# Sequence transform of a three-block model over folded rows, with its table resident, the convolution's norm moved one stage up, and context taps moved to GpSimd

## The chip, the cores and the metric

The kernel runs on one core of one Trainium2 chip. The metric is the device time of one execution in microseconds. Engines are named as in the profile: PE is TensorE, PEld its weight loads, DVE is VectorE, ACT is ScalarE, POOL is GpSimd, SP is SyncE.

## What is computed

The model has three blocks over 1024 tokens of width 1024 (a first block with two mixers and a feed-forward, then an "even" and an "odd" block), with 256 context tokens beside them in the last two. The change touches the even block's mixer alone:

```python
a_val, a_glu, a_gate, b_val, b_gate = split(h @ w_in, [512] * 5)
u = a_val * sigmoid(a_glu)
u = silu(layernorm(dwconv(u, a_conv_w) + a_conv_b, a_ln_g, a_ln_b))   # 31 taps along the tokens
y_a = (u @ a_pw_w + a_pw_b) * silu(a_gate)
y_b = fourier_mix(b_val, b_fw) * silu(b_gate)
return concat([y_a, y_b]) @ w_out

def fourier_mix(v, fw):            # v: (tokens, 4 groups, 128)
    f = fftn(v, axes=(tokens, group width), norm='ortho').real
    return einsum('blgd,gde->blge', f, fw)
```

The same runs for the 1024 tokens (`U`, `VB`) and the 256 context tokens (`UC`, `VBC`). Channels lie on the partitions, tokens along the free axis, so 512 channels are 4 tiles j.

## The kernel before

The program is a row of stages. An engine enters a stage when ACT, PE and DVE have left the one before (`gate`); POOL and SP run ahead of the gate as their own semaphores let them. Two stages matter here.

**Stage `ein`** is the projection h @ w_in: 20 units of 128 output columns. A unit's weights go as RAW through a split into a high part WH and a low part WL; the unit's matmuls (L306 for the 1024 tokens, L313 for the context) wait for WL. From unit 4 on ACT makes WH (L2266), behind its eviction of unit i-2, and POOL makes WL by one subtraction (L2278) in `ein_pool`, in the order of the units. WH and WL have two buffers each, so WL(i) can be made while unit i-1 runs, and no earlier than unit i-2 is done. Units 0 to 7 are glu and value of the four channel tiles; after unit 2j+1 DVE writes U[j] and UC[j] (L2248, L2249), then frees the unit's PSUM. Units 8 to 11 are b_val (`VB`), 12 to 15 b_gate, 16 to 19 a_gate, all evicted by ACT.

Beside this DVE runs the convolution, `conv(dve, a, b)`: for each of 4 x 31 taps q one multiply-add over 1024 tokens into ACC and one over 256 into ACCC (L2230; the first tap of a tile is L2227, the copy back L2235). It does 12 taps after each of the first three pairs of units and the other 88 after the fourth; each tap waits for the one before it.

At the end of `ein`, `val_pe` forms PQ (the 128-point transform times fw, L2367) and multiplies VB and VBC by it: 8 tiles of 128 of the 1024 tokens and 2 of context, 4 groups each, 256 columns (L2377). ACT evicts each tile in two copies (L2391) to VP_, VQ_ (the cosine and the sine side) or VPC, VQC.

**Stage `ef`**: the transform along the tokens. `DFT` lists ("a", t) for groups 0 and 1 and ("b", t) for groups 2 and 3, 8 token tiles each, then two context tiles "c". An "a" or "b" tile is 2 groups x 2 sides of a 512-column f32 matmul (L2436; each f32 matmul is two records in the trace), 64 in all. Even tokens go to one PSUM bank, odd ones to another; outputs k and k + 512 are their sum and difference, made by DVE in `group(g)`. The cosine and sine rows come from a 1024 x 1024 table in 128-row pieces over four buffers (`TAB`), each piece loaded twice, once for "a" and once for "b". In the same stage DVE, ACT and PE do the layer norm of the convolution: sums over the 4 channel tiles (L2529, `ones_sum` L1602), centring (L2534), squares by ACT (L2493), sums of these (L2541, L1602), square root (L2496), reciprocal (L2545), scaling (L2549), silu (L2501). `group(g)` then waits for ACT's copy EV, makes YB (L2556, L2557), gates it (L2560), and splits it (ACT L2510, DVE L2562); `YBC` is the same for the context (L2568 on). Last, four units of the pointwise product (`N_PW`, L2463 and L2468) need all silus, and DVE's sums of groups 0, 1 and the context (`ef_y` 6); units 2 and 3 need the eviction of unit 0 and 1 (L2581), which DVE does behind group 3. Stage `eo` (w_out) follows directly.

Of the kernel before, what the change touches and what calls it, by code (L numbers as in the profile page):

```python
# [14 lines left out]
F32 = mybir.dt.float32  # L15
# [43 lines left out]
def shape_constants():  # L59
# [58 lines left out]
    for length in (SEQ, CTX):  # L118
        tiles = []
        for parity in range(2):  # L120
            for m in range(length // 2 // P):
                l = 2 * (m * P + np.arange(P)) + parity
                a = 2 * np.pi * (np.outer(l, np.arange(length // 2)) % length) / length
                tiles.append(np.concatenate([np.cos(a), np.sin(a)], 1))
        out[f"dft_{length}"] = np.concatenate(tiles).astype(np.float32)
# [9 lines left out]
def build_program(nc, A, out):  # L135

    ctx = ExitStack()
    with ctx:
# [2043 lines left out]

        xe_out = whole("xe_out")
# [25 lines left out]

        def conv(dve, a, b):  # L2210


            for q in range(a, b):
                j, k = divmod(q, CONV_W)
                wk = V[:, VEC["conv_w"] + j * CONV_W + k:VEC["conv_w"] + j * CONV_W + k + 1]
                if k == 0:
                    dve.wait_ge(S("ein_u"), 1 + j + 1)
                    if j:
                        dve.wait_ge(S("ein_cv"), 2 * j)
                for i, (u, acc, T) in enumerate(((U, ACC, SEQ), (UC, ACCC, CTX))):  # L2220
                    tap = S(("ein_tap", "ein_ctap")[i])
                    if q:
                        dve.wait_ge(tap, q)
                        if i == 0:
                            dve.wait_ge(S("ein_ctap"), q)
                    if k == 0:
                        dve.tensor_scalar(acc[:], u[:, j, k:k + T], wk, vec("conv_b", j), ALU.mult, ALU.add)\  # L2227
                           .then_inc(tap, 1)
                    else:
                        dve.scalar_tensor_tensor(out=acc[:], in0=u[:, j, k:k + T], scalar=wk, in1=acc[:], op0=ALU.mult,  # L2230
                                                 op1=ALU.add).then_inc(tap, 1)
                if k == CONV_W - 1:
                    for i, (u, acc, T) in enumerate(((U, ACC, SEQ), (UC, ACCC, CTX))):
                        dve.wait_ge(S(("ein_tap", "ein_ctap")[i]), q + 1)
                        dve.tensor_copy(u[:, j, 0:T], acc[:]).then_inc(S("ein_cv"), 1)  # L2235

        def ein_dve(dve):
# [7 lines left out]
            for j in range(4):  # L2245
# [22 lines left out]
        def ein_pool(pool):  # L2268
            r0, u0 = info("ein")["r0"], info("ein")["u0"]
            for i in range(20):  # L2270
# [1117 lines left out]
```

## Time and profile before

| | us |
|---|---|
| median of 3 runs | 2534.98 (2531.2 to 2537.91) |
| profiled execution | 2531.24 |
| its span, first to last instruction | 2529.5 |
| PE busy | 2385.8 (94%) |
| DVE busy | 1394.4 (55%) |
| POOL busy | 730.2 (29%) |
| ACT busy | 631.4 (25%) |
| mean granted PE clock | 0.982 |

The page's chain that ended last gives PE 80%, DVE 8%, ACT 4%. Times in the text are those of the profiled execution, counted from the start of the span. The two stages lie at 1457.7 to 1729.5 (`ein`, from its third unit on) and 1729.5 to 1827 (`ef`).

### The profile page before, as it was taken

The page shows a single profiled execution, that of the slowest core. Times are in us where ns is not written, and L with a number is a line of the kernel's source. Part 1 is how long each engine was busy: PE and PEld are TensorE (multiplying, and loading weights), DVE is VectorE, ACT ScalarE, POOL GpSimd, SP SyncE. Part 2 cuts the span into 40 slices and gives each one's busy share as a digit, 9 for nine tenths or more (in the row PEclk, how much of TensorE's full clock was granted, in tenths as well). Part 3 has the DMA queues.
Part 4 walks back from the last instruction along what each step waited for, and adds up shares of the span by engine and source line. Part 5 has one row for each costly group of instructions (what it writes and reads, how often), then busy time and mean ns, then how long its engine had stood idle before and what let it go on. Part 6 is the DMA issues. An engine that isn't in the chain of part 4 may idle for free.

```text
span 2529.5 us, 28684 instructions
## 1 busy us (share of the span) xinstructions
PE 2385.8 (94%) x11308; PEld 1893.9 (75%) x11308; DVE 1394.4 (55%) x1621; ACT 631.4 (25%) x949; POOL 730.2 (29%) x492
## 2 busy tenths in 40 slices
PE   5999889999899999999998799999998999999998
PEld 3776656677678888888875488885586788879987
DVE  7567754436624454455446789997428320327733
ACT  4012344523512101100124611214204200014420
POOL 1331330036453332333265021210046233240021
PEclk9999989999999999999999899999999999999999
DMA  6652000132232333233232031113232531110021
GB/s 231 212 173 73 22 19 9 39 103 84 58 117 79 100 105 92 88 108 97 85 115 75 1 108 48 34 32 120 76 117 83 166 84 50 50 33 18 1 92 75
DMA packets 228852, 206.97 MB, mean 82 GB/s; under 512 B 15248, under 2 KB 203280, under 8 KB 227712
## 3 DMA queue, kind: packets, MB, share of 16 engines
q1 hardware_dynamic: 223552, 178.61, 23.4%
q10 hardware_dynamic: 3840, 21.89, 2.2%
q0 software_dynamic: 1344, 4.91, 0.5%
q8 instruction: 75, 1.23, 0.2%
q14 instruction: 41, 0.34, 0.0%
HBM read 180.35 MB, written 17.83 MB: 78 GB/s over the span
## 4 chain that ended last, share of the span: by engine, by line
PE 80%; DVE 8%; ACT 4%; issue 3%; DMA 1%; PEld 1%; POOL 1%; PEldq 1%; SPq 0%; ACTq 0%; DVEq 0%; POOLq 0%
PE G L1730 27%; PE G L306 26%; PE M L3123 3%; PE G L1164 2%; PE M L313 2%; PE G L2620 2%; PE M L1765 1%; PE G L2436 1%; PE M L2436 1%; PE G L2463 1%; PE M L1115 1%; PE M L2622 1%; PE M L3100 1%; POOL WL L283 1%; PE G L2377 1%
## 5 line engine op out<-in xcount | busy, mean ns | idle before, releaser
L280 POOL TENSOR_SCALAR WH<-RAW 128x1024 fp32r<-128x1024 f32 (+1 forms) x156 | 136.0, 872 | 874.4 <-PE G L1730 456.1
L306 PE MATMUL G<-HH,WH 128*128 128x512 f32 x1024 | 321.7, 395 | 15.9 <-DVE HL L494 5.5
L306 PE MATMUL G<-HL,WH 128*128 128x512 f32 x1024 | 316.7, 390 | 0.0
L306 PE MATMUL G<-HH,WL 128*128 128x512 f32 x1024 | 316.2, 390 | 0.0
L283 POOL TENSOR_TENSOR WL<-RAW,WH 128x1024 fp32r<-128x1024 f32 (+1 forms) x156 | 301.1, 1930 | 13.0
L306 PEld LDWEIGHTS G<-HH,WH 128*128 128x128 f32 x1024 | 191.4, 189 | 60.1 <-issue 15.6
L306 PEld LDWEIGHTS G<-HL,WH 128*128 128x128 f32 x1024 | 193.1, 189 | 40.9
L306 PEld LDWEIGHTS G<-HH,WL 128*128 128x128 f32 x1024 | 192.8, 188 | 40.6
L1730 PE MATMUL G<-HH,WH 128*128 128x512 f32 x608 | 209.2, 395 | 11.2 <-POOL WL L283 5.7
L268 POOL TENSOR_SCALAR WH<-RAW 128x1024 fp32r<-128x1024 f32 x52 | 56.1, 1079 | 531.2 <-PE G L306 190.6
L1730 PE MATMUL G<-HL,WH 128*128 128x512 f32 x608 | 206.0, 390 | 0.0
L1730 PE MATMUL G<-HH,WL 128*128 128x512 f32 x608 | 206.0, 390 | 0.0
L1976 DVE TENSOR_TENSOR FLT<-T,FHT 128x1024 fp32r<-128x1024 f32 (+1 forms) x40 | 53.5, 1339 | 259.0 <-ACT FHT L1886 259.0
L1730 PE MATMUL G<-FHT,WH 128*128 128x512 f32 x512 | 170.6, 394 | 9.6 <-issue 5.6
L1960 DVE SCALAR_TENSOR_TENSOR X<-G,MODA,X 128x512 f32<-128x512 f32 (+1 forms) x96 | 97.1, 1012 | 147.9 <-PE G L1730 142.9
L2230 DVE SCALAR_TENSOR_TENSOR ACC<-U,V,ACC 128x1024 f32<-128x1024 f32 x120 | 167.2, 1393 | 13.9 <-DVE UC L2249 1.0
L1882 ACT ACTIVATE T<-G 128x1024 f32<-128x1024 f32 (+1 forms) x40 | 34.2, 855 | 542.6 <-PE G L1730 542.6
L1730 PE MATMUL G<-FLT,WH 128*128 128x512 f32 x512 | 168.4, 390 | 0.0
L1730 PE MATMUL G<-FHT,WL 128*128 128x512 f32 x512 | 168.2, 389 | 0.0
L1730 PEld LDWEIGHTS G<-HH,WH 128*128 128x128 f32 x608 | 114.4, 188 | 37.9 <-issue 7.4
L271 POOL TENSOR_TENSOR WL<-RAW,WH 128x1024 fp32r<-128x1024 f32 x52 | 133.7, 2572 | 4.3
L1730 PEld LDWEIGHTS G<-HL,WH 128*128 128x128 f32 x608 | 114.6, 188 | 25.0 <-issue 1.4
(561 smaller groups left out, 4430.8 us busy)
## 6 DMA issues: line engine op xcount, KB each, us to landing
RAW<-in_w_ff SPq DMA_DIRECT2D x40, 512.0 KB, 3.9
RAW<-in_w_ff SPq DMA_DIRECT2D x80, 256.0 KB, 2.8
WVEC<-in_w_ada SPq DMA_DIRECT2D x24, 512.0 KB, 4.6
FVEC<-in_e_w_mod SPq DMA_DIRECT2D x24, 512.0 KB, 3.8
FVEC<-in_o_w_mod SPq DMA_DIRECT2D x24, 512.0 KB, 4.0
RAW<-in_o_w_in SPq DMA_DIRECT2D x24, 512.0 KB, 3.7
RAW<-in_e_w_in SPq DMA_DIRECT2D x20, 512.0 KB, 3.6
ADA<-in_w_ada SPq DMA_DIRECT2D x4, 2048.0 KB, 18.4
```

Source lines behind the costliest of these rows:

```text
L268: pool.tensor_scalar(WH[s][:], RAW[s][:], 1.0, 0.0, ALU.mult, ALU.add).then_inc(w_high, 1)
L271: pool.tensor_tensor(WL[s][:], RAW[s][:], WH[s][:].bitcast(F32), ALU.subtract).then_inc(w_split[s], 1)
L280: pool.tensor_scalar(hi, raw, 1.0, 0.0, ALU.mult, ALU.add).then_inc(w_high, 1)
L283: pool.tensor_tensor(lo, raw, hi.bitcast(F32), ALU.subtract).then_inc(w_split[U % 2], 1)
L306: m = pe.matmul(G[s][:, n * w:(n + 1) * w], part[s][:, k, :], acts[i][:, k, n * w:(n + 1) * w], start=first, stop=last)
L313: m = pe.matmul(M[s][:, 0:CTX], part[s][:, k, :], side[i][:, k, :], start=k == 0 and part is WH and i == 0, stop=k == KT - 1 and part is WL)
L1164: pe.matmul(G[1][:, cols_], VP[:, kb_, first:first + P], PF[g % 4][:, 0:n], start=(kb_ == 0), stop=(kb_ == 4 * c + 3)).then_inc(S("ml_pv"), 1)
L1730: m = pe.matmul(G[s][:, wf_bank(i) if kind == "o" else half(h)], part[s][:, k, :], moving[:, half(h)], start=(j == 0 and part is WH and mo ...
L1960: dve.scalar_tensor_tensor(out=X[:, f, cc], in0=got, scalar=gate, in1=X[:, f, cc], op0=ALU.mult, op1=ALU.add).then_inc(unit_freed[U % 2], 1)
L1976: dve.tensor_tensor(FLT[k][:, cc], T2[a % 2][:, cc], FHT[k][:, cc].bitcast(F32), ALU.subtract)\
L2230: dve.scalar_tensor_tensor(out=acc[:], in0=u[:, j, k:k + T], scalar=wk, in1=acc[:], op0=ALU.mult, op1=ALU.add).then_inc(tap, 1)
L3123: m = pe.matmul(M[1][:, c0:c0 + HEAD], WPT[i % 2][:, b * P:(b + 1) * P], v, start=(b == 0), stop=(b == len(blocks) + 1))
```

## The change

1. **Folded transform.** Rows l and 1024 - l have the same cosine and opposite sine, so the inputs are folded first: for odd l, and for l = 2 mod 4, POOL forms the difference (`VD`) and the sum (in place in `VB`) of the two rows, in `val_fold`, 4 instructions for each of 4 groups. Rows 0 mod 4 stay. There are then 5 row tiles in place of 8 (two "four", two "odd", one "two"); "four" and "two" have 256 table columns a side, "odd" 512. The 256 columns of "four" and "two" are joined to 512 by two more DVE instructions in each `group(g)`, after an ACT copy `EVT` of the "two" part.
2. **Resident table.** The five pieces (`FOUR`, `ODD`, `TWO`, and `DFC` for the context) are each loaded once: two in the RAW buffers, three after the gate of `ef`.
3. **Norm begun in `ein`.** Sums, centring, squares and their sums go from `ef` to the end of `ein`: DVE behind `conv`, ACT's squares between the evictions of `val_act`, the two `ones_sum` in `val_pe`, the first ahead of PQ, the second behind the last tile.
4. **Context taps on POOL.** For channel tiles 0 to 2 the context's 93 taps go to POOL, as a product (TENSOR_SCALAR with a tap weight, 128x256) and an addition (TENSOR_TENSOR) each, 7 taps behind each WL from unit 5 on (`context_taps`). Tile 3's context taps stay on DVE with their accumulator in PSUM (`ACC3`). DVE does 16 taps, not 12, behind each of the first three pairs.

```diff
+        TMPC = [at(f"TMPC{s}", [P, CTX], F32, sel_at + s * kb) for s in range(2)]
+        ACC3 = M[0][:, 512:512 + CTX]
...
-                for i, (u, acc, T) in enumerate(((U, ACC, SEQ), (UC, ACCC, CTX))):
+                parts = ((U, ACC[:], SEQ),) if j < 3 else ((U, ACC[:], SEQ), (UC, ACC3, CTX))
+                for i, (u, acc, T) in enumerate(parts):
                     tap = S(("ein_tap", "ein_ctap")[i])
-                    if q:
+                    if q and i == 0:
                         dve.wait_ge(tap, q)
-                        if i == 0:
-                            dve.wait_ge(S("ein_ctap"), q)
+                    if k and j == 3:
+                        dve.wait_ge(S("ein_ctap"), k)
...
+        def context_taps(pool, a, b):
+            def product(q):
+                j, k = divmod(q, CONV_W)
+                if k:
+                    pool.wait_ge(S("ein_cacc"), q - 1)
+                    pool.tensor_scalar(TMPC[q % 2][:], UC[:, j, k:k + CTX], tap_weight(j, k), None, ALU.mult)\
+                        .then_inc(S("ein_cmul"), 1)
+            product(a)
+            for q in range(a, b):
+                j, k = divmod(q, CONV_W)
+                if k == 0:
+                    pool.wait_ge(S("ein_u"), 1 + j + 1)
...
+                if q + 1 < b and k + 1 < CONV_W:
+                    product(q + 1)
+                if k:
+                    pool.wait_ge(S("ein_cacc"), q)
+                    pool.wait_ge(S("ein_cmul"), q - j)
+                    pool.tensor_tensor(ACCC[:], TMPC[q % 2][:], ACCC[:], ALU.add).then_inc(S("ein_cacc"), 1)
...
                 if j < 3:
-                    conv(dve, step, step + 12)
-                    step += 12
+                    conv(dve, step, step + 16)
+                    step += 16
             conv(dve, step, 4 * CONV_W)
+            dve.wait_ge(S("ein_cv"), 5)
+            dve.wait_ge(S("ein_pcv"), 3)
+            for i, (u, acc, _, T) in enumerate(sums_of):
+                for j in range(1, 4):
...
+            dve.wait_ge(S("ef_mean"), 1)
...
@@ ein_pool
                 pool.wait_ge(w_split[U_ % 2], U_ // 2 + 1)
                 pool.sem_inc(raw_used[r % 2], 1)
+                if 10 <= i < 14:
+                    val_fold(pool, i - 10)
+                if i >= 5:
+                    context_taps(pool, min(7 * (i - 5), 3 * CONV_W), min(7 * (i - 4), 3 * CONV_W))
...
+        def val_fold(pool, j):
+            pool.wait_ge(S("ein_m"), 8)
+            pool.wait_ge(S("ein_a"), 9 + 2 * j)
+            for at_, n, first, step in ((0, 2 * P, 1, 2), (2 * P, P, 2, 4)):
+                low = VB[:, j, first:first + step * (n - 1) + 1:step]
+                high = VB[:, j, SEQ - first:SEQ - first - step * (n - 1) - 1:-step]
+                pool.tensor_tensor(VD[:, j, at_:at_ + n], low, high, ALU.subtract).then_inc(S("val_d"), 1)
+                pool.wait_ge(S("val_d"), 2 * j + 1 + at_ // (2 * P))
+                pool.tensor_tensor(low, low, high, ALU.add).then_inc(S("val_s"), 1)
...
@@ val_pe
+            pe.wait_ge(S("ef_sum"), 6)
+            ones_sum(pe, M[0], SEQ, [AR])
+            ones_sum(pe, M[1], CTX, [ARC]).then_inc(S("ef_mean"), 1)
...
+            pe.wait_ge(S("ef_acc"), 6)
+            ones_sum(pe, M[1], SEQ, [AR])
+            ones_sum(pe, M[0], CTX, [ARC])
@@ val_act
+                for i, j in ([(0, t)] if t < 4 else [(1, 0), (1, 1)] if t == 4 else [(1, t - 3)]):
+                    u, _, sq, T = sums_of[i]
+                    act.wait_ge(S("ef_cen"), 4 * i + j + 1)
+                    if j >= 2:
+                        act.wait_ge(S("ef_acc"), 3 * i + 1)
+                    act.activation(sq[j % 2][:], u[:, j, 0:T], ACT.Square).then_inc(S("ef_sq"), 1)
...
@@ ef_sp
+            load_unit(sp, r0 // 2, 0, A["dft_four"].rearrange("(t p) n -> p t n", p=P), FOUR)
+            load_unit(sp, r0 // 2, 1, A["dft_odd"][0:P, :], ODD[0])
+            gate(sp, current[0])
+            sp.dma_start(ODD[1], A["dft_odd"][P:2 * P, :]).then_inc(tab_loaded, 16)
+            sp.dma_start(TWO[:], A["dft_two"]).then_inc(tab_loaded, 16)
+            sp.dma_start(DFC[:].rearrange("p t n -> p (t n)"), A["dft_c"]).then_inc(tab_loaded, 16)
...
@@ ef_pe
+                for g in ((0, 1) if kind == "a" else (2, 3)):
+                    to = ef_bank(part == "odd", g)
+                    to = to[:, 256:512] if part == "two" else to[:, 0:w]
+                    for q, vv in enumerate((VP_, VQ_)):
+                        m = pe.matmul(to, vv[:, t, g * P:(g + 1) * P], tab[:, q * w:(q + 1) * w],
+                                      start=(q == 0 and i == 0), stop=(q == 1 and (i == 1 or part == "two")))
...
@@ ef_dve, group(g)
+                dve.tensor_tensor(EV[g % 2][:, 0:256], four, EVT[g % 2][:], ALU.add).then_inc(S("ef_even"), 1)
+                dve.scalar_tensor_tensor(out=EV[g % 2][:, 256:512], in0=EVT[g % 2][:], scalar=-1.0, in1=four,
+                                         op0=ALU.mult, op1=ALU.add).then_inc(S("ef_even"), 1)
+                dve.wait_ge(S("ef_even"), 2 * g + 2)
```

## Rows read from the trace of the kernel before

**Rows 1.** Table of stretches: us, then PE, PEld, DVE, ACT, POOL busy, PE clock, DMA share, GB/s.

```profile
1457.70:1706.00 248.30, 248.30 (x1296) 214.00 (x1296) 230.88 (x243) 36.53 (x45) 41.99 (x17) 1.00 0.17 55
```

**Rows 2.** The chain that ended last, 1690 to 1830: start us, us, what.

```profile
1703.14 2.88 PE M L313 x24
...
1707.53 2.04 PE M L2367 x16
...
1710.73 17.56 PE G L2377 x80
...
1729.48 7.13 PE G L2436 x16
1736.61 2.15 PE M L1602 x6
...
1775.24 3.57 PE G L2428 x32
...
1792.55 6.87 PE G L2463 x16
...
1801.15 6.87 PE G L2463 x16
```

**Rows 3.** The timeline of DVE in `ein`: start us, us, what.

```profile
1500.98 0.48 DVE L2230 SCALAR_TENSOR_TENSOR ACCC<-UC,V,ACCC 128x256 f32<-128x256 f32 x1
1501.57 1.28 DVE L2230 SCALAR_TENSOR_TENSOR ACC<-U,V,ACC 128x1024 f32<-128x1024 f32 x1
1502.77 2.62 DVE L2230 SCALAR_TENSOR_TENSOR ACCC<-UC,V,ACCC 128x256 f32<-128x256 f32 x1
```

**Rows 4.** The same timeline, the convolution's last instruction.

```profile
1723.65 0.28 DVE L2235 COPY UC<-ACCC 128x256 f32<-128x256 f32 x1
```

**Rows 5.** The timeline of POOL in `ein`.

```profile
1486.87 2.39 POOL L2278 TENSOR_TENSOR WL<-RAW,WH 128x1024 fp32r<-128x1024 f32 x1 [9.98 <-ACT WH L2266]
1502.34 2.77 POOL L2278 TENSOR_TENSOR WL<-RAW,WH 128x1024 fp32r<-128x1024 f32 x1 [13.08 <-ACT WH L2266]
```

**Rows 6.** The timeline of all engines near 75 us, another stage.

```profile
75.52 1.05 POOL L280 TENSOR_SCALAR WH<-RAW 128x1024 fp32r<-128x1024 f32 x1 [7.68 <-PE G L306]
75.54 2.09 DVE L391 SCALAR_TENSOR_TENSOR WSUM<-WVEC,CACT,WSUM 128x1024 f32<-128x1024 f32 x1 [0.53 <-DMA WVEC<-in_w_ada]
...
76.65 3.23 POOL L283 TENSOR_TENSOR WL<-RAW,WH 128x1024 fp32r<-128x1024 f32 x1
```

**Rows 7.** Groups by line and form, POOL: busy us, mean ns.

```profile
L1004 POOL TENSOR_TENSOR WQS<-WUQN,WQS 128x256 fp32r<-128x256 f32 x1 | 0.8, 775 | 0.0
...
L1000 POOL TENSOR_SCALAR WQS<-WUQN 128x256 fp32r<-128x256 f32 x1 | 0.4, 402 | 0.0
```

**Rows 8.** The timeline of DVE near 589 us (M is in PSUM).

```profile
589.25 4.28 DVE L1997 SCALAR_TENSOR_TENSOR X<-M,X 128x512 f32<-128x512 f32 x7
```

**Rows 9.** The timeline of POOL near 589 us.

```profile
589.65 2.41 POOL L283 TENSOR_TENSOR WL<-RAW,WH 128x1024 fp32r<-128x1024 f32 x1
```

**Rows 10.** The timeline of ACT, 1712 to 1751.

```profile
1712.77 0.60 ACT L2391 ACTIVATE EVP<-G 128x512 f32<-128x512 f32 x1 [2.09 <-PE G L2377]
...
1740.14 2.10 ACT L2493 ACTIVATE ASQ<-U 128x1024 f32<-128x1024 f32 x2 [10.75 <-DVE U L2534]
...
1750.79 1.28 ACT L2496 ACT_TABLE_LOAD   x1
```

**Rows 11.** The timeline of DVE in `ef`.

```profile
1755.83 6.55 DVE L2545 RECIPROCAL AR<-AR 128x1024 f32<-128x1024 f32 x1 [4.38 <-ACT AR L2496]
...
1768.57 1.43 DVE L2549 TENSOR_TENSOR UC<-UC,ARC 128x256 f32<-128x256 f32 x4
1772.42 0.69 DVE L2556 TENSOR_TENSOR YB<-G,EV 128x512 f32<-128x512 f32 x1 [2.42 <-ACT EV L2508]
...
1777.42 0.69 DVE L2556 TENSOR_TENSOR YB<-G,EV 128x512 f32<-128x512 f32 x1
```

**Rows 12.** The same table, a short stretch in another stage.

```profile
1995.30:1998.70 3.40, 3.40 (x6) 1.49 (x5) 0.25 (x1) 0.03 (x1) 0.00 (x0) 0.51 0.54 124
```

More of the change, by code:

```diff
@@ L117, in shape_constants, with table @@
     out["dft_d"] = out["dft_d"].astype(np.float32)
[L118 to L125, printed above, removed]
+    def table(l, k, length):
+        a = 2 * np.pi * (np.outer(l, np.arange(k)) % length) / length
+        return np.concatenate([np.cos(a), np.sin(a)], 1).astype(np.float32)
+    q = np.arange(P)
+    out["dft_four"] = table(4 * np.arange(2 * P), SEQ // 4, SEQ)
+    out["dft_two"] = table(4 * q + 2, SEQ // 4, SEQ)
+    out["dft_odd"] = table(2 * np.arange(2 * P) + 1, SEQ // 2, SEQ)
+    out["dft_c"] = np.concatenate([table(2 * q + parity, CTX // 2, CTX) for parity in range(2)], 1)
     return out
@@ L2349, in build_program @@
-        DFT = [("a", t) for t in range(NT)] + [("b", t) for t in range(4)] + [("c", 0), ("c", 1)] + \
-            [("b", t) for t in range(4, NT)]
+        N_VAL = N_FOLD + 2
+        FOLD = [("four", 0), ("four", 1), ("odd", 0), ("odd", 1), ("two", 0)]
+        DFT = [("a", t) for t in range(N_FOLD)] + [("b", t) for t in range(4)] + [("c", 0), ("c", 1), ("b", 4)]
         N_PW = 4
-        dft_raw = [i for i in range(len(DFT)) if i % 4 < 2]
         def val_tile(t):
-            if t < NT:
-                return (VB, VP_, VQ_, t) + divmod(t, NT // 2)
-            return VBC, VPC, VQC, t - NT, t - NT, 0
+            if t < N_FOLD:
+                return (VB, VP_, VQ_, t)
+            return VBC, VPC, VQC, t - N_FOLD
@@ new lines, in val_rows @@
+        def val_rows(t, g):
+            if t >= N_FOLD:
+                rows = VBC[:, g, t - N_FOLD:t - N_FOLD + 2 * P - 1:2]
+                return rows, rows
+            kind, i = FOLD[t]
+            if kind == "four":
+                rows = VB[:, g, 4 * P * i:4 * P * i + 4 * P - 3:4]
+                return rows, rows
+            first, step = (2 * P * i + 1, 2) if kind == "odd" else (2, 4)
+            at_ = P * i if kind == "odd" else 2 * P
+            return VB[:, g, first:first + step * (P - 1) + 1:step], VD[:, g, at_:at_ + P]
@@ L2454, in ef_pe @@
+                if t == N_FOLD - 1:
+                    m.then_inc(S("ef_a" if kind == "a" else "ef_b"), 1)
+                elif kind == "b" and t in (1, 2):
+                    m.then_inc(raw_used[t - 1], 1)
+            for u in DFT:
+                transform(*u)
+            r0 += 2
             for j in range(N_PW):
```

198 lines of the change are left out of this document (86 added, 112 removed).

## The prediction

> **What bounds the kernel now.** I read the table of stretches first, then the chain that ended last, then the timelines of DVE and POOL. In `ein` PE is busy in all 248.3 us of the stretch, DVE in 230.9 and POOL in only 42.0 [rows 1]. The chain says the same from 1690 to 1827 with hardly a gap: a unit of the projection (10.9 us of L306, 2.9 of L313, 13.78 in all), PQ, ten value tiles in 17.56 us, then the transform, the two sums, the context tiles and the pointwise product [rows 2]. So PE is the bound of both stages, and DVE is close behind: its convolution ends at 1723.9 [rows 4], 5.5 us ahead of the end of `ein`. POOL looks free. The reader should see that it isn't free for DVE: a context tap of DVE takes 0.48 us, but 2.62 when it meets POOL's WL, which started at 1502.34 and ended at 1505.11, and that WL itself took 2.77 instead of 2.39, because it had to wait for the tap in flight, 1501.57 to 1502.85 [rows 3, 5].
>
> **The rule of POOL against DVE.** The cleanest rows are three: POOL's one-input WH ran 75.52 to 76.57; DVE's multiply-add with two SBUF inputs, issued at 75.54, ended at 77.63, so 1.06 after POOL; POOL's WL, issued at 76.65, ended at 79.88, 2.25 after DVE [rows 6]. The two engines never overlap, POOL's one-input instruction blocks too, and when both wait they alternate instruction by instruction. Each hides some 0.14 us (POOL, 2.39 against 2.25) or 0.2 (DVE, 1.28 against 1.06) of its start in the wait. A DVE instruction with an input in PSUM is not held: seven of L1997 take 4.28 us, 0.6 each, though a WL of 2.41 us lies in them [rows 8, 9].
>
> **Part 4, the context taps on POOL, is the costly one.** A product (one input) is priced by the 128x256 row at 0.40, an addition at 0.78 [rows 7]; with 0.08 between POOL's instructions (76.57 to 76.65, rows 6) a tap costs POOL 1.34 us alone. The weight is read from SBUF here and is a constant in the row; I take the same price. While DVE always has a tap waiting, each of the two instructions waits one DVE tap: 1.07 + 0.26 + 1.07 + 0.64 = 3.04 us. Seven of these are 21.3, and a WL is 1.07 + 2.25 = 3.3, so a step of `ein_pool` is 24.6 us where PE needs one WL every 13.78. Queued behind the taps on POOL is the next WL, and behind that PE. In the old trace POOL was idle there.
>
> Now the sum, from WL(5), which ends at 1489.3, 1486.87 + 2.39 [rows 5], to WL(14), nine steps later. A POOL instruction that meets a DVE tap costs 0.85 more than alone (1.07 less the hidden 0.14 and the 0.08).
> (a) Three steps, until unit 7 lets DVE go on: DVE has only its 2 x 16 taps. 3 x (7 x 1.34 + 2.47) + 32 x 0.85 = 62.8.
> (b) From there DVE has 45 taps of tiles 1 and 2 left (93 less 48), which meet the 49 instructions of three steps. Two steps of 24.6, and a third with a fold. A fold is four two-input instructions, two of 256 and two of 128 elements, 0.78 and (estimate, half of the slope) 0.52 each: 4 x 1.07 + 2 x 0.64 + 2 x 0.38 = 6.3. Together 24.6 + 24.6 + 30.9 = 80.1.
> (c) Three steps with folds, against DVE's tile 3. There each main tap is followed by a context tap with its accumulator in PSUM, which holds nobody, so every second POOL instruction meets a tap: solo 14.6 + 9.5 x 0.8 = 22 each, 66.
> Sum 208.9: WL(14) at 1698.2. PE would want it at 1706.0 less 6 units of 13.78, at 1623.3. PE's end of `ein`'s units is **74.9 us later**. By then DVE has done its taps, so the remaining steps take POOL 11.9 us, under 13.78, and the delay stays what it is. PE stands idle some 7 us ahead of unit 14; a stretch of 3.4 us at a granted clock of 0.51 exists [rows 12], and if the next unit starts so it loses 1.7. Bounds: 57 and 93 us, from POOL prices 15% down and 20% up and from the clock's loss nil or twice. The wait of the unit evictions on DVE (16 taps at some 1.5 us are 24.5 us in a pair of 27.6) fits.
>
> The Trainium skill (GPSIMD Engine Reference, Performance pitfalls for Q7 kernels) says that a GpSimd read whose step is over 8 bytes costs about half as much again per element. No row shows a strided GpSimd read. By it the two short instructions of a fold, step 4 words, would take some 0.15 us more each, about 1 us in all up to WL(14); the sum above leaves it out.
>
> **Part 3, the norm in `ein`.** DVE gets to the sums when POOL's taps are done, step 18, about 30 us ahead of unit 19's end; so the first `ones_sum` finds them ready. From unit 19's end: eviction 1.5 (1706.0 to 1707.5), `ones_sum` 2.15, PQ and its copies 3.20, first tile to its copy 2.0 [rows 2, 10]. Then ACT leads: seven tiles of two copies at 1.1 (the copy at 0.60, overlapping), four squares at 1.05, four short ones at 0.37, say 14 with the gaps; then the last addition 0.5 and `ones_sum` 2.4. Sum 25.8, against 23.5 before (1706.0 to 1729.5). So **+2.3**, though PE's own value work falls from 17.6 to some 13 us. Bounds 0 and +6: ACT's squares hidden wholly, or each wait of ACT on DVE's sums exposed.
>
> **Parts 1 and 2, the transform.** A 512-column f32 matmul costs 0.858 (13.73 for 16 of them), a 256-column one 0.44 (17.56 for 40) [rows 2]. Before: 64 x 0.858 = 54.9, plus 4.3 for the two sums and 3.6 for context. After: 2 x (12 x 0.44 + 8 x 0.858) = 24.3 plus 3.6. PE alone would win 35 us, but now another wait is last. The pointwise product needs `ef_y` 6. DVE: table load 1.28 and the square root 1.1 on ACT [rows 10], then reciprocal to scaling 1755.83 to 1770.0, 14.2 us [rows 11], so 16.6 after the gate; groups 0 and 1 at 5.0 each (1772.42 to 1777.42, rows 11) plus 0.8 for the two added instructions, 28.2; the context's sums 1.3: the product starts at 29.5, where PE's own work would have allowed 27.8. It runs 4 x 8.60 = 34.4 (1792.55 to 1801.15, rows 2); its third unit wants DVE's first eviction, which comes at 16.6 + 3 x 5.8 + 4.9 + 5.8 + 1.8 = 46.5, and starts at 46.7. End at 63.9, against 97.5 before (1729.5 to 1827.0). **-33.6.** Bounds -38 (DVE's chain shorter by ACT and DVE overlap) and -27 (the evictions late for units 3 and 4, or the three late table loads slower than the 6.9 us that PE spends on the two early ones). The loads' cover is that work; moved bytes are a third of before. After `eo` begins nothing changes.
>
> **How it adds up.** Profiled execution 2531.2 + 74.9 + 1.7 + 2.3 - 33.6 = 2576.5; the median of the runs lies 3.7 above the profiled one, so **2580 us**, slower by 1.8%.
>
> **The rivals.**
> *GpSimd's taps run beside DVE's* (faster). If 256-element instructions with a weight from SBUF didn't exclude DVE, a step is 11.9 us, PE never waits, DVE's convolution ends near 1661, and only the last two parts count: 2531.2 + 2.3 - 33.6 + 3.7 = 2504. It decides from the point at which a step costs less than 13.78. Against it: the held tap and the held multiply-add [rows 3, 6]. 8%.
> *Only two-input GpSimd instructions exclude* (no change). Then a tap costs 1.07 + 0.64 + 0.56 = 2.3, a step 19; by the same three phases the delay is near 30, and the total 2531.2 + 30 - 31.3 + 3.7 = 2534. Against it: the one-input WH held DVE for 0.8, 2.09 less 1.28 [rows 3, 6]. 5%.
> *POOL waits longer than for one DVE tap* (slower still). If it is passed over now and then, one in four of its 110 instructions that meet a tap up to WL(14) (32 + 49 + 28) waits 1.07 more: 29 us, 2609. No row speaks for it. 7%.
> Forecast: 80%.
>
> The Trainium skill (SBUF, two separate sides) has the first rival decided: the pair of ports that both engines share goes to one instruction as a whole. It doesn't say who is next when both wait; rows 6 alternate. Were it always GpSimd, with 11.9 of its 13.78 us a step, DVE would get one or two taps a step, and the convolution would end near 1820, some 110 us late for the first `ones_sum`; that stays out.
>
> **How the numbers follow.** The bounds of the parts, not all at one end together, put the likeliest case at 2550 to 2602. The range is that; left out are the two cases below it, 13%, and most of the one above. About 0.3%, 8 us, is what a measurement of this kernel can tell from no change. Faster 0.10, within 0.05, slower 0.85. Predicted 2580, range 2548 to 2602.
>
> **What would show it.** Right: DVE's L2230 in the first half of `ein` at 1.5 to 2.3 us instead of 1.28; POOL's 256-element instructions at 1.2 to 1.8; POOL busy nearly throughout `ein` from unit 3 to unit 13; PE idle ahead of L306, released by WL, in units 7 to 14, and the last unit ending near 1781; `ef` some 34 us shorter, with PE waiting for YBC before L2463. Wrong: PE without gaps in `ein`, or POOL's products short while DVE taps run. I would be most wrong if POOL's tap with a weight from SBUF is far from 1.34 us.

## The result and the profile after

| | before | after |
|---|---|---|
| median, us | 2533.09 | 2601.86 (2599.17 to 2614.06) |
| ratio | | 1.0282, interval 1.0264 to 1.0301 |
| profiled execution, its span, us | 2531.24, 2529.5 | 2602.83, 2601.0 |
| PE busy, granted clock | 2385.8, 0.982 | 2378.0, 0.964 |
| DVE, ACT, POOL busy | 1394.4, 631.4, 730.2 | 1361.7, 625.8, 971.9 |

The change makes the kernel 2.8% slower; the forecast was 1.8% (2580 us). 2601.86 us is the upper end of the range given (2602), and as a ratio above it: 2602 to the 2534.98 of the kernel before is 1.0264. PE is busy for 8 us less and ends 72 us later, so the loss is idle time. The waits of PE in the stretch of `ein` (for whom: us in total, times, longest) say whom it waited for; the kernel before has no wait for WL there:

```profile
PE G L308 <- POOL WL L2333: 77.4, 12, 17.7
```

The table of stretches over the same units (rows 1 are the answer of before, with the same columns). POOL goes from 42 us in 248 to 284 in 343, and the granted clock from 1.00 to 0.88:

```profile
1460.50:1803.30 342.80, 265.32 (x1296) 225.38 (x1296) 218.39 (x174) 36.42 (x45) 284.25 (x219) 0.88 0.12 40
```

The chain that ended last, 1755 to 1900 (start us, us, what). Where before it was PE nearly alone [rows 2], it now comes through POOL's taps and WL, and returns to PE for the last two units only:

```profile
1756.07 0.93 POOL TMPC L2251
...
1758.52 2.36 POOL WL L2333
...
1773.07 2.35 POOL WL L2333
...
1775.64 11.07 PE G L308 x48
1786.71 2.87 PE M L315 x24
1789.59 10.91 PE G L308 x48
```

The last unit's matmuls end at 1803.3; before they ended at 1706.0. POOL's instructions at work in `ein`, by line and form (busy us, mean ns | idle before us), and DVE's main tap, which answers to the 1.28 of rows 3:

```profile
L2251 POOL TENSOR_SCALAR TMPC<-UC,V 128x256 f32<-128x256 f32 x90 | 121.8, 1357 | 7.8 <-POOL WL L2333 1.9
L2267 POOL TENSOR_TENSOR ACCC<-TMPC,ACCC 128x256 f32<-128x256 f32 x90 | 94.7, 1052 | 1.2
L2333 POOL TENSOR_TENSOR WL<-RAW,WH 128x1024 fp32r<-128x1024 f32 x16 | 42.1, 2630 | 25.7 <-ACT WH L2321 25.7
...
L2237 DVE SCALAR_TENSOR_TENSOR ACC<-U,V,ACC 128x1024 f32<-128x1024 f32 x120 | 184.1, 1534 | 7.0 <-DVE UC L2284 0.7
```

**The balance of the two spans**, 71.6 us: the units of `ein` end 94.5 us later, besides 2.8 us by which the stage already began later in code that is the same; from there to the gate of `ef` 25.7 us against 23.5, +2.2; `ef` 67.8 us against 97.5, -29.7; and 1.8 in the stages behind it, again the same code.

### The profile page after: what moved, and what is told of

The parts are those of the page before. It is cut to its first block, busy times and chain, and to the rows that moved or that the text cites. A ratio compares the mean times of both kernels' runs of the same rounds, so it can differ in the third digit from the quotient of the medians.

```text
span 2601.0 us, 28685 instructions
## 1 busy us (share of the span) xinstructions
PE 2378.0 (91%) x11260; PEld 1898.7 (73%) x11260; DVE 1361.7 (52%) x1533; ACT 625.8 (24%) x943; POOL 971.9 (37%) x694
## 4 chain that ended last, share of the span: by engine, by line
PE 68%; POOL 11%; DVE 8%; issue 5%; ACT 4%; PEld 2%; DMA 2%; PEldq 1%; SPq 0%; ACTq 0%; POOLq 0%; DVEq 0%
PE G L1732 27%; PE G L308 19%; POOL TMPC L2251 4%; POOL ACCC L2267 3%; PE M L3190 3%; PE G L1166 2%; PE G L2687 2%; POOL WL L2333 1%; PE M L1767 1%; PE G L2558 1%; PE M L1117 1%; PE M L2689 1%; PE M L3167 1%; PEldq L3355 1%; POOL WL L285 1%
## 5 line engine op out<-in xcount | busy, mean ns | idle before, releaser
L308 PE MATMUL G<-HH,WH 128*128 128x512 f32 x1024 | 328.4, 403 | 91.5 <-POOL WL L2333 77.4
L308 PE MATMUL G<-HL,WH 128*128 128x512 f32 x1024 | 321.9, 396 | 0.0
L1732 PE MATMUL G<-HH,WH 128*128 128x512 f32 x608 | 209.2, 395 | 11.2 <-POOL WL L285 5.6
L1732 PE MATMUL G<-HL,WH 128*128 128x512 f32 x608 | 206.3, 390 | 0.0
L2237 DVE SCALAR_TENSOR_TENSOR ACC<-U,V,ACC 128x1024 f32<-128x1024 f32 x120 | 184.1, 1534 | 7.0 <-DVE UC L2284 0.7
```

Source lines behind the costliest of these rows:

```text
L308: m = pe.matmul(G[s][:, n * w:(n + 1) * w], part[s][:, k, :], acts[i][:, k, n * w:(n + 1) * w], start=first, stop=last)
L1732: m = pe.matmul(G[s][:, wf_bank(i) if kind == "o" else half(h)], part[s][:, k, :], moving[:, half(h)], start=(j == 0 and part is WH and mo ...
L2237: dve.scalar_tensor_tensor(out=acc, in0=u[:, j, k:k + T], scalar=tap_weight(j, k), in1=acc, op0=ALU.mult, op1=ALU.add).then_inc(tap, 1)
```

## The experiments

Theory A, the forecast's: POOL's instructions and DVE's taps hold the same way into SBUF by turns, so the 93 context taps make POOL the bound of `ein`, and the rest of the change is a gain. The main rival: what the change does to PE directly (the clock, the folds, the transfers) costs the time. Delays of the units below are net of how late unit 3 of the stage began.

**1. Part 4 alone.** The kernel before with the context taps of tiles 0 to 2 on POOL and 16 taps of DVE a pair, and nothing of parts 1 to 3.

```diff
 ...
                 pool.sem_inc(raw_used[r % 2], 1)
+                if i >= 5:
+                    context_taps(pool, min(7 * (i - 5), 3 * CONV_W), min(7 * (i - 4), 3 * CONV_W))
```

> The kernel before with part 4 alone: context taps of tiles 0 to 2 on POOL, 16 taps of DVE behind a pair; no fold, old transform, norm in its old stage. Theory A: POOL's steps from unit 5 on are as long as in the changed kernel but for the fold (6.7 us in each of three contested steps and 3.0 in one), so the units end 94.5 - 23 = 71 us late and nothing is won back: 2600 to 2608. Rival B (the exclusion matters only together with the fold): below 2580.

Measured: 2613.04 us (2611.03 to 2615.88), ratio 1.0324 (1.0303 to 1.0346), slower than the whole change. Its units end 81 us late, and its table of stretches gives `ef` as long as before:

```profile
1811.50:1908.70 97.20, 97.20 (x269) 48.38 (x269) 58.76 (x62) 28.01 (x36) 5.76 (x6) 1.00 0.35 117
```

So part 4 by itself costs all that is lost and more, a little above the range expected, as its units are 81 us late and not 71. The whole change delays the units by 94.5, 13.6 more than part 4 alone: that is what the four folds on POOL add. Three of them meet DVE's taps (the first takes 6.5 us, 1606.57 to 1613.10, the other two 6.7) and one doesn't (3.1), 23 us of work, of which 13.6 reach the path. In the next experiment, where POOL has time to spare, the folds delay nothing.

**2. The change without its context taps on POOL.** DVE does all of them, with the accumulator in PSUM as the change has it for tile 3, 12 taps behind a pair; the folds, the table and the norm stay as changed. The edit does one thing more: each tap now waits only for the last tap of its own accumulator, while in the kernel before, and in tile 3 of the change, a main tap also waits for the context tap ahead of it (`ein_ctap`). The same holds of the context taps that DVE does in experiments 4 to 7.

```diff
-                    if q and i == 0:
-                        dve.wait_ge(tap, q)
-                    if k and j == 3:
-                        dve.wait_ge(S("ein_ctap"), k)
...
+                    parts.append((UC, 0, ACC[:, 0:CTX] if PSUM_ACC else ACC3, CTX, "ein_ctap", c, c + 1))
+                for u, o, acc, T, tap, before, _ in parts:
+                    if before > 0:
+                        dve.wait_ge(S(tap), before)
...
-                if i >= 5:
-                    context_taps(pool, min(7 * (i - 5), 3 * CONV_W), min(7 * (i - 4), 3 * CONV_W))
```

> The changed kernel with all context taps back on DVE, with 12 taps behind a pair of units; fold, resident table and norm as in the change. Theory A (POOL's taps cost the whole loss): PE has no gap before its L308 units; DVE's convolution ends near 1732, as before plus some 8 us of the fold's 16 instructions, and the first sum over the tiles then waits for it, some 27 us behind the last unit; against that stand the 30 us that the folded transform saves, so the time is 2528 to 2538, no change from before. Rival B (the folded stage itself is slower than thought, or POOL's taps cost less than the whole): over 2550, or under 2515.

Measured: 2514.58 us (2505.43 to 2522.3), ratio 0.9921 (0.9894 to 0.9949): faster than the kernel before, and by more than I expected. PE has no gap over the units (247 us of 247), and waits for the convolution only at the first `ones_sum`:

```profile
1467.00:1713.60 246.60, 246.60 (x1289) 212.63 (x1288) 232.80 (x259) 36.47 (x45) 66.98 (x32) 1.00 0.16 51
```
```profile
PE M L1604 <- DVE ARC L2302: 5.8, 1, 5.8
```

No unit is late without POOL's taps, so these are the whole loss, as Theory A said. The time is below Theory A's range all the same, and 0.4 us inside the range of rival B (under 2515). The expectation had DVE's convolution end near 1732; it ended at 1714.4. That isn't the place of the accumulator: with the sums in PSUM a context tap takes 475 ns on the average against 622 before, but a main tap 1527 against 1393, and all taps together 240 us against 242. It is the wait that the edit leaves out. DVE's timeline late in the convolution:

```profile
1707.05 1.27 DVE L2241 SCALAR_TENSOR_TENSOR ACC<-U,V,ACC 128x1024 f32<-128x1024 f32 x1
1708.25 0.47 DVE L2241 SCALAR_TENSOR_TENSOR M<-UC,V,M 128x256 f32<-128x256 f32 x1
1708.64 1.27 DVE L2241 SCALAR_TENSOR_TENSOR ACC<-U,V,ACC 128x1024 f32<-128x1024 f32 x1
```

Main taps start 1.59 us apart here and 1.79 in the kernel before (1635.41 and 1637.20). Over the 88 taps behind the fourth pair, which take 161.5 us from first start to last in place of 178.9, this is 17 us. With the wait kept the first sum would come some 17 us later (an estimate from these rows), the time would be near 2532, and nearly all of the 19 us gained here would be gone. So this run doesn't show that parts 1 to 3 alone are a gain; its `ef`, 67.4 us against 97.5, does show that the stage is.

**3. What the tap's weight costs.** The change with the product's weight a constant in the instruction in place of a value read from SBUF; it leaves out the real weights, and so computes another convolution of the context.

```diff
-                    pool.tensor_scalar(TMPC[q % 2][:], UC[:, j, k:k + CTX], tap_weight(j, k), None, ALU.mult)\
+                    pool.tensor_scalar(TMPC[q % 2][:], UC[:, j, k:k + CTX], 0.03, 0.0, ALU.mult, ALU.add)\
```

> The changed kernel, but POOL's context products multiply by the constant 0.03 and not by the tap weight read from SBUF, so the context's convolution of tiles 0 to 2 is wrong in its values. Theory A (what the forecast mis-sized is the price of a product whose weight is read from SBUF: 0.93 us in the changed kernel's trace, 0.40 forecast): the product falls to 0.40, a tap alone from 1.73 to 1.34, POOL's steps behind unit 14 from 14.5 to 11.9 us, below PE's 13.78, and the delay of the unit stage from 94.5 to about 75; time 2580 to 2585. Rival B (the product is slow for another reason, its f32 output or the operand's place): the product stays at 0.93 and the time at 2602.

Measured: 2589.85 us (2578.01 to 2594.89), ratio 1.0215 (1.0178 to 1.0251), the units 79 us late: the product falls as Theory A said, the time lies between the two theories. POOL's timeline when DVE is idle, first that of the change, then this kernel's:

```profile
1721.82 0.93 POOL L2251 TENSOR_SCALAR TMPC<-UC,V 128x256 f32<-128x256 f32 x1
1722.71 0.74 POOL L2267 TENSOR_TENSOR ACCC<-TMPC,ACCC 128x256 f32<-128x256 f32 x1
```
```profile
1727.38 0.41 POOL L2251 TENSOR_SCALAR TMPC<-UC 128x256 f32<-128x256 f32 x1
1727.87 0.74 POOL L2267 TENSOR_TENSOR ACCC<-TMPC,ACCC 128x256 f32<-128x256 f32 x1
```

The weight read from SBUF costs 0.52 us: 0.93 against 0.41, which is the 0.40 of rows 7. Against DVE's main taps alone (tiles 0 to 2) it costs next to nothing. The timeline of the change there, then this kernel's:

```profile
1498.21 1.78 POOL L2251 TENSOR_SCALAR TMPC<-UC,V 128x256 f32<-128x256 f32 x1
1499.96 1.26 POOL L2267 TENSOR_TENSOR ACCC<-TMPC,ACCC 128x256 f32<-128x256 f32 x1
1501.32 1.78 POOL L2251 TENSOR_SCALAR TMPC<-UC,V 128x256 f32<-128x256 f32 x1
```
```profile
1501.15 1.26 POOL L2251 TENSOR_SCALAR TMPC<-UC 128x256 f32<-128x256 f32 x1
1502.49 1.59 POOL L2267 TENSOR_TENSOR ACCC<-TMPC,ACCC 128x256 f32<-128x256 f32 x1
1504.17 1.26 POOL L2251 TENSOR_SCALAR TMPC<-UC 128x256 f32<-128x256 f32 x1
```

From product to product it is 3.11 with the weight (1498.21 to 1501.32) and 3.02 with the constant. So the extra half microsecond passes beside DVE's tap. Beside tile 3, where DVE alternates a main tap and a context tap in PSUM, it is another matter. This kernel's POOL and one main tap of DVE there:

```profile
1641.60 1.26 POOL L2251 TENSOR_SCALAR TMPC<-UC 128x256 f32<-128x256 f32 x1
1642.94 0.73 POOL L2267 TENSOR_TENSOR ACCC<-TMPC,ACCC 128x256 f32<-128x256 f32 x1
1643.10 1.66 DVE L2237 SCALAR_TENSOR_TENSOR ACC<-U,V,ACC 128x1024 f32<-128x1024 f32 x1
1643.77 1.26 POOL L2251 TENSOR_SCALAR TMPC<-UC 128x256 f32<-128x256 f32 x1
```

With the short product the addition begins before DVE's next main tap and takes its time as alone, and DVE waits for it (1.66 instead of 1.28): a tap of POOL costs 2.17 us (1641.60 to 1643.77). With the weight it costs 3.58 (experiment 8 has the rows).

The 15 us by which this kernel's units end earlier all lie ahead of WL(14): three phases of three steps take 61.3, 76.1 and 72.5 us against 65.0, 80.4 and 79.7. The first two gain in the main by taps that met no DVE tap, the third in tile 3. Behind WL(14) both need 86 us, for different reasons. The change is held by POOL's steps there, at the full clock. This kernel's steps are short enough (11.6), and PE runs without a wait, but its first 14 us after the idle time have a mean granted clock of 0.77:

```profile
1702.20:1716.00 13.80, 13.47 (x47) 11.06 (x48) 0.00 (x0) 0.00 (x0) 12.14 (x19) 0.77 0.19 56
```

**4. All main sums in PSUM.** The main accumulator moves to two unused halves of PSUM banks, so a main tap becomes two instructions of 512 columns with one SBUF input each; tile 3's context accumulator takes the old one's place in SBUF. POOL's work is as in the change.

```diff
+                for n in range(halves):
+                    w = SEQ // halves
+                    acc = M[n][:, 512:1024] if PSUM_ACC else ACC[:]
+                    parts.append((U, n * w, acc, w, "ein_tap", halves * (q - 1) + n + 1, halves * q + n + 1))
...
-                        dve.scalar_tensor_tensor(out=acc, in0=u[:, j, k:k + T], scalar=tap_weight(j, k), in1=acc,
-                                                 op0=ALU.mult, op1=ALU.add).then_inc(tap, 1)
+                        dve.scalar_tensor_tensor(out=acc, in0=u[:, j, o + k:o + k + T], scalar=tap_weight(j, k), in1=acc,
+                                                 op0=ALU.mult, op1=ALU.add).then_inc(S(tap), 1)
```

> The changed kernel with DVE's main accumulator in PSUM, two halves of 512 tokens in the free banks of M, so that no tap of DVE reads two SBUF tensors; POOL does what it did. Theory A (the loss is the mutual exclusion): POOL's product stays near 0.93 and its addition near 0.74 throughout, DVE's half taps near 0.68; a step of POOL is 14.7 us, with a fold 17.8, so PE is delayed by 13 to 20 us and not by 94, and DVE's convolution ends before 1680; time 2515 to 2525. Rival B (POOL's instructions are slow in this stage whatever DVE does): 2590 or more.

Measured: 2525.15 us (2517.35 to 2526.45), ratio 0.9964 (0.9951 to 0.9976), with POOL's taps all where the change put them. Their durations are those of an uncontested POOL, in the groups by line and form:

```profile
L2256 POOL TENSOR_SCALAR TMPC<-UC,V 128x256 f32<-128x256 f32 x90 | 83.3, 930 | 7.8 <-POOL WL L2339 1.9
L2273 POOL TENSOR_TENSOR ACCC<-TMPC,ACCC 128x256 f32<-128x256 f32 x90 | 66.6, 740 | 1.2
L2339 POOL TENSOR_TENSOR WL<-RAW,WH 128x1024 fp32r<-128x1024 f32 x16 | 38.8, 2426 | 29.5 <-ACT WH L2327 29.5
```
```profile
PE G L308 <- POOL WL L2339: 9.3, 5, 3.7
```

1357 ns falls to 930, 1052 to 740, and PE's waits for WL from 77.4 us to 9.3. This settles that most of the 94.5 us comes from POOL and DVE excluding each other and not from the number of POOL's instructions, which alone delays the units by some 14 us: a step takes 14.6 us (WL ended at 1511.71 and at 1526.27), more than PE's 13.78, and with a fold 17.8. Experiment 7 tells the place of the sums from the halving.

**5. The same, with two tiles of context taps on POOL, five taps a step.** A step is then near 11 us, and VectorE has 31 context taps more.

```diff
-                    context_taps(pool, min(7 * (i - 5), 3 * CONV_W), min(7 * (i - 4), 3 * CONV_W))
+                    context_taps(pool, min(5 * (i - 5), 2 * CONV_W), min(5 * (i - 4), 2 * CONV_W))
```

> The main taps of VectorE sum into PSUM in two halves as in e4_sums_in_psum, and GpSimd takes the context's taps of two tiles (62, five per step) instead of three (93, seven per step); VectorE takes tiles 2 and 3 of the context. Theory A (GpSimd's own work per step, the products and additions at 0.93 and 0.74 us, is what delays the units once the port is free): a step of GpSimd is 2.43 + 5 x 1.67 = 10.8 us, under TensorE's 13.8, and 14 to 15 us only where a fold lies in it, so no unit waits long; the 9.3 us of waiting of e4 go, the units end 10 to 15 us earlier than there, and the time is 2503 to 2513 us. Theory B (what delayed e4 was VectorE's longer taps or something else beside GpSimd): VectorE has 31 more taps of 0.48 us to do, the units end no earlier than in e4, and the time is 2522 to 2535 us.

Measured: 2504.77 us (2501.47 to 2513.73), ratio 0.9886 (0.9865 to 0.9907), the fastest of all. PE has no gap over the units, and its wait for WL is gone from the list:

```profile
1460.50:1708.20 247.70, 247.70 (x1296) 213.59 (x1294) 218.32 (x334) 36.47 (x45) 153.49 (x157) 1.00 0.17 55
```

The units end within 0.5 us of where PE alone puts them, as A said. DVE's convolution ends 20.7 us ahead of them, so the wait left out in the 62 pairs of this kernel (some 12 us at 0.2 each, an estimate) doesn't decide here. No unit of `ein` is late here, so parts 1 to 3 are what the 26 us against the kernel before come from.

**6. The same, with no taps on POOL at all**, and 12 taps of DVE behind a pair (edit against experiment 5).

```diff
-                if i >= 5:
-                    context_taps(pool, min(5 * (i - 5), 2 * CONV_W), min(5 * (i - 4), 2 * CONV_W))
```

> All sums of the convolution, the main's in two halves, lie in PSUM and VectorE does all taps; GpSimd has its weights and the four folds alone. VectorE's work in the stage: 124 x (2 x 0.72 + 0.48) = 238 us, against 228 in e2_context_taps_on_dve, and none of it holds the port of the low parts of the weights against GpSimd. Theory A: the units end where TensorE alone puts them, as in the kernel before, or up to 5 us earlier since the low parts are no longer held up by VectorE's taps; the convolution ends 0 to 10 us later than the units, and the sums of the norm wait for it; 2508 to 2520 us. Theory B (the port costs the units nothing when GpSimd has little to do): same as e2_context_taps_on_dve or up to 10 us later, 2514 to 2526 us.

Measured: 2519.62 us (2516.94 to 2528.46), ratio 0.9946 (0.9924 to 0.9967). The two expectations overlap here and the time lies in both. The trace says what it is: the units aren't late, but DVE's convolution ends 10 us behind them and PE waits for the first sum,

```profile
PE M L1604 <- DVE ARC L2302: 15.3, 1, 15.3
```

so some context taps do belong on POOL, once DVE's main sums let it work. That is the whole distance to experiment 5: 15 us.

**7. Main taps in halves, accumulators in SBUF.** A test of how the turns are dealt out: the same elements contested, in twice as many instructions.

```diff
-                    acc = M[n][:, 512:1024] if PSUM_ACC else ACC[:]
+                    acc = ACC[:, n * w:(n + 1) * w]
```

(against the kernel of experiment 4; the context accumulator of tile 3 goes back to PSUM.)

> The kernel after with each main tap of VectorE as two instructions of 512 columns, accumulators in SBUF as they are; GpSimd's work is unchanged. Theory A (a GpSimd instruction waits until the VectorE instruction under way has ended, and VectorE's next one goes after it): the wait is for half as long an instruction, so a contested tap of GpSimd falls from 3.10 us to 2.2 to 2.5 us, the contested tap against VectorE's tile 3 likewise, the units are delayed by 45 to 65 us instead of 94.6, and the time is 2545 to 2575 us. Theory B (the two engines share the port evenly by time or by element, whatever the length of an instruction): a contested tap stays at 3.0 to 3.2 us, and the time is 2595 to 2612 us. VectorE's own taps become longer, 1.5 to 1.7 us, in both.

Measured: 2565.22 us (2560.73 to 2570.31), ratio 1.0136 (1.011 to 1.0162), the units 58 us late. The timeline of POOL, late in the convolution:

```profile
1653.05 1.24 POOL L2256 TENSOR_SCALAR TMPC<-UC,V 128x256 f32<-128x256 f32 x1
1654.26 0.73 POOL L2273 TENSOR_TENSOR ACCC<-TMPC,ACCC 128x256 f32<-128x256 f32 x1
1655.09 1.24 POOL L2256 TENSOR_SCALAR TMPC<-UC,V 128x256 f32<-128x256 f32 x1
```

A tap takes 2.04 us (1653.05 to 1655.09) instead of 3.10, a little less than Theory A's 2.2. So a turn is one instruction, of 1024 columns or of 512. DVE pays for it: its 240 halves take 1106 ns on the average, 2.2 us a main tap against 1.53 (1.5 to 1.7 expected), and the convolution ends at 1747.9 instead of 1692.4. Of PE's waits in the units 31.7 us are for WL, and 10.0 are one wait for DVE, which frees a unit's PSUM late.

**8. Tile 3's context taps behind its main taps.** A test of the stretch in which the forecast was furthest off.

```diff
-                parts = ((U, ACC[:], SEQ),) if j < 3 else ((U, ACC[:], SEQ), (UC, ACC3, CTX))
...
+            if b < 4 * CONV_W:
+                return
+            j = 3
+            for k in range(CONV_W):
+                if k:
+                    dve.wait_ge(S("ein_ctap"), k)
+                    dve.scalar_tensor_tensor(out=ACC3, in0=UC[:, j, k:k + CTX], scalar=tap_weight(j, k), in1=ACC3,
+                                             op0=ALU.mult, op1=ALU.add).then_inc(S("ein_ctap"), 1)
...
```

> The kernel after with VectorE's 31 context taps of tile 3 behind its 31 main taps instead of between them. Theory A (between them VectorE issues two instructions per period and the one that sums in PSUM leaves GpSimd no turn of its own, so that a tap of GpSimd costs two periods of 1.79 us, 3.58 us, there): with main taps alone beside it a tap costs 3.10 us again, the low part that ended 79.7 us after WL11 ends 68 to 72 us after it, the units end 8 to 11 us earlier, 2590 to 2596 us. VectorE's convolution ends later, up to 1705 us, and nothing waits for that. Theory B (GpSimd is slower there for another reason, the low clock or the transfers): no change of more than 3 us, 2598 to 2606 us.

Measured: 2602.49 us (2600.73 to 2605.39), ratio 1.0274 (1.0253 to 1.0295), in the time no difference from the change (1.0282): the total lies in the range of Theory B. The timelines speak for the mechanism of Theory A. That of the change, DVE and POOL together in tile 3, then this kernel's POOL at the same place:

```profile
1649.90 1.28 DVE L2237 SCALAR_TENSOR_TENSOR ACC<-U,V,ACC 128x1024 f32<-128x1024 f32 x1
1650.10 1.88 POOL L2251 TENSOR_SCALAR TMPC<-UC,V 128x256 f32<-128x256 f32 x1
1651.10 0.48 DVE L2237 SCALAR_TENSOR_TENSOR M<-UC,V,M 128x256 f32<-128x256 f32 x1
1651.69 1.28 DVE L2237 SCALAR_TENSOR_TENSOR ACC<-U,V,ACC 128x1024 f32<-128x1024 f32 x1
1651.95 1.62 POOL L2267 TENSOR_TENSOR ACCC<-TMPC,ACCC 128x256 f32<-128x256 f32 x1
1652.89 0.48 DVE L2237 SCALAR_TENSOR_TENSOR M<-UC,V,M 128x256 f32<-128x256 f32 x1
1653.48 1.28 DVE L2237 SCALAR_TENSOR_TENSOR ACC<-U,V,ACC 128x1024 f32<-128x1024 f32 x1
1653.67 1.88 POOL L2251 TENSOR_SCALAR TMPC<-UC,V 128x256 f32<-128x256 f32 x1
```
```profile
1655.69 1.78 POOL L2256 TENSOR_SCALAR TMPC<-UC,V 128x256 f32<-128x256 f32 x1
1657.44 1.24 POOL L2272 TENSOR_TENSOR ACCC<-TMPC,ACCC 128x256 f32<-128x256 f32 x1
1658.78 1.77 POOL L2256 TENSOR_SCALAR TMPC<-UC,V 128x256 f32<-128x256 f32 x1
```

In the change a tap of POOL takes two of DVE's pairs (1650.10 to 1653.67, 3.57 us), and here 3.09, as A said and as in tiles 0 to 2. The three steps up to WL(14) take 73.6 us instead of 79.7. That is 6 and not the 8 to 11 of the expectation, since only some 11 of POOL's taps lie beside tile 3: the third step comes when DVE has ended. The units end some 5 us earlier net of the start; in the execution with the trace the stages behind `ef`, the same code, took 5.2 us more than in the change, so the total doesn't show it.

## Why the forecast fell short

**Right: what bounds, what becomes the bound, and the gains.** POOL became the bound of `ein`, and PE waited for its WL 12 times. The price of a contested tap in tiles 0 to 2 was 3.10 us (forecast 3.04), of a contested fold 6.5 (6.3), and the WL under contention 3.32 (3.3). That the tap came so near is in part luck: its product was priced 0.53 too low, of which only 0.09 shows there (experiment 3). The steps (a) and (b), WL(5) to WL(11), took 65.0 + 80.4 = 145.4 us (forecast 142.9). The first rival, that POOL's taps run beside DVE's, is out for sums in SBUF; experiment 4 shows that it is what happens with sums in PSUM. The rival by which only two-input instructions of POOL exclude is out too: it had 2.3 us for a contested tap. The stretch to the gate cost 2.2 us more (2.3).

**Wrong, step (c): 66 forecast, 79.7 measured**, 13.7 of the 17.9 us by which the units' delay was too small (94.5 against 74.9 + 1.7; its upper bound was 93). Step by step it was 34.4, 28.1 and 17.2 against 22 each. The forecast said that the context tap of tile 3, which sums in PSUM, "holds nobody, so every second POOL instruction meets a tap". The timeline above shows that every one meets a tap. DVE isn't slowed in it (1.28 and 0.48, as alone): each POOL instruction goes in the half microsecond of the PSUM tap, and when it is done, at 1651.98 for the product of 1650.10, DVE's next main tap (1651.69) has begun. A pair has a gap for one POOL instruction, so a tap of POOL costs two pairs, 3.58 us. Experiment 8 takes the pairs away and the price goes back to 3.09. Experiment 3 keeps the pairs and shortens the product, and the price is 2.17: with the product of 0.40 us that the forecast had, every second POOL instruction does meet a tap. So what failed here is the price of the product, carried into a place where it decides whether the addition still fits. The two folds beside the pairs add to it, 6.7 us each where the forecast's sum has 4.2 (2.6 alone and two meetings of 0.8). The third step was too dear in the forecast, since DVE had ended; without that the miss would be 4.8 us larger. Neither experiment brings the three steps to 66: they take 72.5 and 73.6. The term needed the row of one pair set against the length of one POOL instruction; I had only averaged.

**Wrong, the price of the product: 0.40 forecast, 0.93 measured.** The row I took has a constant and the new instruction a weight from SBUF, and the forecast said that it would be most wrong there. Beside main taps alone it hardly matters, in tile 3 it does (both experiment 3). Behind WL(14) it does too: a step was to take 11.9 us, under PE's 13.78, so that the delay would stay what it was. The timeline after gives 14.53 (WL(14) ended 1717.26, WL(18) 1775.40), 0.75 over PE's 13.78, four times: 3.0 us. The chain shown with the result has POOL on it until WL(18), which is this. I put the 2.2 us of step (a) down to the same price, in its taps that meet no DVE tap; experiment 3, which takes the price away, shortens the three steps of (a) by 3.8.

**Wrong, the clock: +1.7 forecast, none in the units of the change.** The clock did fall to its lower level, 1.2 GHz, after PE had stood idle, far oftener than the 3.4 us I allowed: between 1656.9 and 1677.4 the table of stretches gives

```profile
1656.90:1677.40 20.50, 5.32 (x13) 4.17 (x14) 19.35 (x22) 1.32 (x2) 19.72 (x13) 0.50 0.09 26
```

But a slow unit of PE fills time in which it would have waited for WL. PE's 1296 matmuls were busy for 265.3 us in place of 248.3, 17.0 more, and the delay of 94.5 is these 17 and the 77.4 of waiting; both are inside POOL's steps. As soon as POOL lets go, the clock does count: in experiment 3 it costs 2.8 us behind WL(14) (the first unit there takes 16.57 against 13.78). In all the forecast of the units missed 2.2 + 0.4 + 13.7 + 3.0 - 1.7 = 17.6 of the 17.9.

**Wrong, `ef`: -33.6 forecast, -29.7 measured.** It came in two parts. The pointwise product started 31.4 us behind the gate (29.5): the forecast spaced groups 0 and 1 by 5.8, the 5.0 of before and 0.8 for the two added instructions, and they came 8.0 apart, since ACT's copy HH of the first stands in ACT's queue behind the silu of U and UC. The silus themselves began late, at 1844.5, with the first U scaled by 1840.6: the change puts the copies EVT ahead of them, and these waited for the transform until 1842.5. DVE's timeline in the change:

```profile
1845.41 0.42 DVE L2619 TENSOR_TENSOR EV<-G,EVT 128x256 f32<-128x256 f32 x1
...
1852.08 1.23 DVE L2629 TENSOR_TENSOR HL<-YB,HH 128x1024 fp32r<-128x1024 f32 x1 [3.33 <-ACT HH L2586]
1853.40 0.42 DVE L2619 TENSOR_TENSOR EV<-G,EVT 128x256 f32<-128x256 f32 x1
```

And its first unit took 8.64 us instead of 6.87 (mean granted clock 0.75 in its first 6.8 us), after PE had stood idle for 2.33 us. That isn't the rule: in experiments 4 to 7 PE waited there as long, 2.3 to 2.4 us, and the unit took 6.95 us at the full clock, so why the clock fell in the change and in experiments 2, 3 and 8 stays open. The order of ACT is read from the trace and not tried by itself; experiments 2 and 5 show the same order.

The rest of the difference, 4.6 us (2.8 ahead of `ein`, 1.8 behind `ef`), lies in code that is the same. The same code behind `ef` took between 697 and 712 us in the profiled executions of the experiments, and nothing here tells why.

**The two pages cited.** The Trainium skill (SBUF, two separate sides) names the condition for the exclusion, two SBUF inputs of VectorE or a two-port mode, and that whoever starts first keeps the pair to the end of its instruction. Experiment 4 agrees with the condition (930 and 740 ns, as alone) and experiment 7 with the second part (2.04 us instead of 3.10). Its "for the whole instruction" doesn't hold of the recorded time of the product with a weight from SBUF, whose extra 0.52 us passes beside DVE's tap. The rule of half as much again for strided reads (GPSIMD Engine Reference, Performance pitfalls for Q7 kernels), weighed ahead of the result, now has a row. The last fold of the change, which met no tap of DVE:

```profile
1701.23 0.85 POOL L2443 TENSOR_TENSOR VB<-VB 128x256 f32<-128x256 f32 x1
1702.04 0.67 POOL L2441 TENSOR_TENSOR VD<-VB 128x128 f32<-128x128 f32 x1
```

With step 4 words 128 elements take 0.67, against my estimate of 0.52 for contiguous ones, so the rule's direction is right; with step 2 words, just inside the rule's 8 bytes, 256 elements take 0.85 against the 0.74 of POOL's addition. For the fold that met no tap that is some 0.5 us in all; the sum could leave it out.

## What to carry to other kernels

Before work goes to an idle GpSimd, look at what VectorE runs beside it: against multiply-adds with two SBUF inputs each GpSimd instruction waits for a whole VectorE instruction (1.55 us each here, 1.02 with halves), and against sums in PSUM it runs at its own speed, which took this kernel from 2.8% slower to 0.4% faster, and to 1.1% faster with only as many taps as fit below TensorE's period. Compare the engine's period with the bound's in every phase, the last and uncontested one too, where 0.75 us over it was paid four times. Weigh the parts of a change by themselves: the transform, the table and the norm were worth about 26 us where nothing in `ein` was late (experiment 5), and the fourth part hid it. And look for the second thing that a test's edit does: in experiment 2 a wait left out of DVE's taps was worth as much as the gain.

## What was not expected of the hardware

- A GpSimd product over 128x256 takes 0.93 us with its scalar read from SBUF and 0.41 with a constant; the extra is covered beside main taps alone (3.10 against 3.02 us a tap) and not beside tile 3 (3.58 against 2.17).
- VectorE's pair of a tap in SBUF (1.28) and one in PSUM (0.48) beside GpSimd isn't slowed at all, while GpSimd, with a product of 0.93 us, gets one instruction a pair, and its tap takes 3.58 us instead of 3.10. More room on VectorE's side made GpSimd slower.
- Halving VectorE's instructions moves the cost from GpSimd (3.10 to 2.04 us a tap) to VectorE (1.53 to 2.2 us a main tap).
- The lower clock of TensorE after its waits cost nothing while it waited for GpSimd (17 us of slower running inside the same delay), but 1.8 us in `ef` and 2.8 us in experiment 3, where TensorE was the bound again. The same wait of 2.3 us ahead of the pointwise product cost 1.8 us in the change and next to nothing in experiments 4 to 7.
- VectorE's pairs start 1.59 us apart when a main tap doesn't wait for the context tap ahead of it, and 1.79 when it does, with the instructions just as long.
